# The opening in four column quarters, the rotary angles moved, later modulation pieces spread by a plan, and attention heads in two banks

## The reference, cut to what matters

```
mod = silu(c) @ ada_w[l] + ada_b[l]            # 2048 x 6144 weights per layer
shift, scale, gate = split(mod, 3)
h = rms_norm(x, norm_g[l]) * (1 + scale) + shift
z = h @ w_in[l]
q_lat, kv_lat, k_rope, mla_gate, conv_in, conv_gate = split(z)   # 512, 256, 64, 1024, 2048, 1024
q, k, v = from rms_norm(q_lat) @ w_q_up, rms_norm(kv_lat) @ w_kv_up, and rotated k_rope
attn = causal attention over 8 heads;  mla_out = attn * silu(mla_gate)
u = glu(conv_in);  u = depthwise conv, 31 taps;  layer norm, silu;  u @ w_pw;  * silu(conv_gate)
x = x + gate * (concat(mla_out, conv_out) @ w_out[l])
```

## Time and profile before

| what | value |
|---|---|
| median of 3 runs | 2290.51 us (2286.9 to 2291.76) |
| the profiled execution | 2290.56 us |
| its span, from first to last instruction | 2288.8 us |
| TensorE busy | 2152.4 us, 94% |
| VectorE busy | 1720.2 us, 75% |
| ScalarE busy | 974.0 us, 43% |
| TensorE's granted clock, mean | 0.973 of full speed |
| moved | 559.4 MB, mean 244 GB/s |

### The profile page before, as it was taken

How to read it: one execution, slowest core, us unless ns; L and a number is a source line. 1 busy time by engine, 2 the same in 40 slices (tenths; PEclk the granted TensorE clock), 3 DMA queues, 4 the chain that set the end, 5 groups by cost and what they waited for, 6 DMA issues and landing times.

```text
span 2288.8 us, 39558 instructions
## 1 busy us (share of the span) xinstructions
PE 2152.4 (94%) x15465; PEld 2040.6 (89%) x15465; DVE 1720.2 (75%) x2347; ACT 974.0 (43%) x1517; POOL 214.1 (9%) x130
## 2 busy tenths in 40 slices
PE   2389999999999999999999999989999999999997
PEld 2389997889999978999999998889999999988886
DVE  6999997797899977878866886787776666654554
ACT  2145445225544353354454444455544444433443
POOL 0000580000007600032000000000000000000000
PEclk7599999999999999999999999999999999999999
DMA  9989956796998487979937995568876555566663
GB/s 337 349 282 351 310 168 214 268 327 200 315 354 257 142 294 244 307 174 304 364 99 255 377 370 166 157 194 270 272 220 198 181 181 181 183 220 184 188 194 123
DMA packets 390355, 559.40 MB, mean 244 GB/s; under 512 B 25543, under 2 KB 316943, under 8 KB 389724
## 3 DMA queue, kind: packets, MB, share of 16 engines
q1 hardware_dynamic: 386304, 550.70, 73.2%
q0 software_dynamic: 1456, 4.28, 0.8%
q10 hardware_dynamic: 2476, 2.82, 0.4%
HBM read 555.57 MB, written 2.18 MB: 244 GB/s over the span
## 4 chain that ended last, share of the span: by engine, by line
PE 80%; DVE 7%; DMA 5%; issue 3%; ACT 3%; SPq 0%; ACTq 0%; DVEq 0%
PE gemm L1688 75%; DMA w_raw<-in_w_in 3%; DMA ada_first<-in_ada_w 2%; DVE w_lo L1161 1%; ACT w_hi L777 1%; DVE ada_even L1129 1%; PE stat L1712 1%; PE bankO L1767 1%; DVE ada_odd L1129 1%; DVE ada_acc L1148 1%; PE bankS L1873 0%; PE bankS L1874 0%; DVE scr L1201 0%; PE bankT L1778 0%; PE gemm L1955 0%
## 5 line engine op out<-in xcount | busy, mean ns | idle before, releaser
L1688 PE MATMUL gemm<-h_hi,w_hi 128*128 128x256 f32 (+1 forms) x3312 | 947.5, 286 | 24.0 <-DVE h_lo L1206 19.0
L1161 DVE TENSOR_TENSOR w_lo<-w_raw,w_hi 128x1024 fp32r<-128x1024 f32 x540 | 654.6, 1225 | 388.6 <-ACT w_hi L777 387.1
L1688 PE MATMUL gemm<-h_lo,w_hi 128*128 128x256 f32 (+1 forms) x3312 | 942.9, 285 | 0.0
L1688 PE MATMUL gemm<-h_hi,w_lo 128*128 128x256 f32 (+1 forms) x3312 | 942.8, 285 | 0.0
L777 ACT ACTIVATE w_hi<-w_raw 128x1024 fp32r<-128x1024 f32 (+1 forms) x604 | 620.3, 1041 | 689.3 <-PE gemm L1688 494.7
L1688 PEld LDWEIGHTS gemm<-h_hi,w_hi 128*128 128x128 f32 (+1 forms) x3312 | 637.9, 193 | 26.7 <-issue 22.0
L1688 PEld LDWEIGHTS gemm<-h_lo,w_hi 128*128 128x128 f32 (+1 forms) x3312 | 638.0, 193 | 0.6
L1688 PEld LDWEIGHTS gemm<-h_hi,w_lo 128*128 128x128 f32 (+1 forms) x3312 | 637.8, 193 | 0.3
L1129 DVE SCALAR_TENSOR_TENSOR ada_even<-ada_raw,c_act,ada_even 128x1024 f32<-128x1024 f32 x160 | 212.9, 1331 | 5.5 <-DMA ada_raw<-in_w_ada 2.3
L651 POOL TENSOR_TENSOR w_lo<-w_raw,w_hi 128x1024 fp32r<-128x1024 f32 x64 | 160.7, 2518 | 412.4 <-ACT w_hi L777 412.3
L1129 DVE SCALAR_TENSOR_TENSOR ada_odd<-ada_raw,c_act,ada_odd 128x1024 f32<-128x1024 f32 x128 | 171.9, 1343 | 6.0 <-DMA ada_raw<-in_ada_w 2.9
(11 more groups left out here) (333 smaller groups left out, 2680.4 us busy)
## 6 DMA issues: line engine op xcount, KB each, us to landing
w_raw<-in_w_in SPq DMA_DIRECT2D x264, 512.0 KB, 6.1
w_raw<-in_w_up SPq DMA_DIRECT2D x176, 512.0 KB, 3.6
ada_raw<-in_ada_w SPq DMA_DIRECT2D x160, 512.0 KB, 7.3
ada_raw<-in_w_ada SPq DMA_DIRECT2D x160, 512.0 KB, 6.1
w_raw<-in_w_out SPq DMA_DIRECT2D x96, 512.0 KB, 6.2
w_raw<-in_w_down SPq DMA_DIRECT2D x88, 512.0 KB, 3.7
ada_first<-in_ada_w SPq DMA_DIRECT2D x32, 512.0 KB, 8.8
ada_late<-in_w_ada SPq DMA_DIRECT2D x32, 512.0 KB, 5.2
```

The costliest lines, as they stand in the source:

```text
L1161: dve.tensor_tensor(w_lo[:, fixed % PARTS, 0:sz], w_raw[:, fixed % RAW, 0:sz], w_hi[:, fixed % PARTS, 0:sz].bitcast(F32), ALU.subtract).th ...
L1688: last = pe.matmul(half(g, k, q), left, right, start=(kt == 0 and j == 0 and (q == 0 or g.wide)), stop=(u == len(g.units) - 1 and t == nk ...
```

## The change

It has six parts.

1. Groups 0 and 1 of layer 0 are read in four quarters: 16 pieces each, a piece with 512 columns of the shift and 512 of the scale. In each quarter VectorE adds 12 pieces to `first_acc`, and TensorE takes every fourth in 8 matmuls of 16 columns (`first_piece`), then adds VectorE's sum (`first_reduce`). `first_tiles` makes the four tiles of h that these columns allow.
2. lat and krope of layer 0 become one product `first`, over k by quarters, in four PSUM banks. SP loads its weights behind each quarter of pieces.
3. ACT issues 8 further small parameter loads at the start and the other 29 after the root of the first norm (`late_consts`); the form of c for quarters is loaded behind x.
4. The rotary angles are computed behind ua.
5. The pieces of groups 2, 3 and 4 ride elsewhere: group 2 on ua and ub; groups 3 and 4 by the table `SPREAD` on kv, q, pw, outca, outcb and outm of layer 0. outm of layer 0 has one body of 8 blocks instead of a loop over 4.
6. Scores and outputs of the attentions alternate between two banks each, `wts` are made in step 0, and out2a waits by tile. The transposes of the opening use two banks in turn.

The core of the diff:

```diff
+QUARTERS = 4
+FROWS = DM // P
+BY_PE = 4
+LEAD = 3
+PAR_EARLY = 10
+SPREAD = {"kv": [1, 0, 1, 0, 1, 0, 1, 0], "q": [2, 1, 1, 1, 2, 1, 1, 1], "pw": [1] * 8,
+          "outca": [3, 2, 2, 2, 3, 2, 2, 2], "outcb": [2] * 8, "outm": [1] * 8 + [0] * 8}
...
+        score_banks = [bankS, banks_g[0][1]]
+        o_banks = [bankO, banks_g[1][1]]
...
 # SP
+            def ada_load_first(qt, j):
+                m = FROWS * qt + j
+                slot = m % FSLOTS
+                if m >= FSLOTS:
+                    if m % BY_PE == BY_PE - 1:
+                        sp.wait_ge(first_by_pe, (m - FSLOTS) // BY_PE + 1)
+                    else:
+                        sp.wait_ge(ada_used, (m - FSLOTS + 1) - (m - FSLOTS + 1) // BY_PE)
...
-            for n in range(2):
-                for j in range(AU):
...
+            for qt in range(QUARTERS):
+                for j in range(FROWS):
+                    ada_load_first(qt, j)
+                load_first(qt)
...
 # ACT
+            act.dma_start(c16_raw[:], a["c"][0].rearrange("(k j) -> k j", j=FROWS)).then_inc(c_loaded, 16)
...
             norm_root(0, scr)
...
+            tr_copy(PAR_FIRST, par[:, 0:par_first])
+            late_consts()
...
+            for qt in range(QUARTERS):
+                first_high(qt, 0)
+                first_high(qt, 1)
+                for t in range(KQ * qt, KQ * (qt + 1)):
+                    act.wait_ge(t_ready, t + 1)
+                    act.activation(h_hi[:, t, :], scr[:, t, :], ACT.Identity, bias=mod[:, 0, t:t + 1]).then_inc(h_hi_ready, 1)
+                first_high(qt, 2)
+                first_high(qt, 3)
+                if qt == 1:
+                    par_copies()
...
 # VectorE
+            for qt in range(QUARTERS):
+                for v, j in enumerate([j for j in range(FROWS) if j % BY_PE != BY_PE - 1]):
+                    if v == LEAD and qt:
+                        first_tiles(qt - 1)
+                    first_piece(qt, j)
+            first_tiles(QUARTERS - 1)
...
                 through(G["ua", l], lambda i, k: value_of_u(i, k, G["ua", l]))
+                if l == 0:
+                    rope_angles()
...
+                    if h < NHA:
+                        head_weights(2 * h)
+                        head_weights(2 * h + 1)
                     if h == NHA + 1:
                         head_low(NHA - 1)
                 if step == 1:
                     if 1 <= h <= NHA:
                         head_scaled(h - 1)
-                    if h < NHA:
-                        head_weights(2 * h)
-                        head_weights(2 * h + 1)
...
 # TensorE
+            def first_piece(qt, j):
+                m = FROWS * qt + j
...
+                pe.wait_ge(ada_loaded[slot], 16 * (m // FSLOTS + 1))
+                for t in range(2 * KQ):
+                    last = pe.matmul(first_sums(qt)[:, t * SUM_COLS:(t + 1) * SUM_COLS],
+                                     first_slot(slot)[:, 0, t * P:(t + 1) * P], c16[:, j, :],
+                                     start=(j == BY_PE - 1 and t == 0), stop=False, skip_group_check=True)
+                last.then_inc(first_by_pe, 1)
...
+            for j in by_pe:
+                first_piece(0, j)
             norm_first(scr)
...
+            first_reduce(0)
+            for qt in range(QUARTERS):
+                more = list(by_pe) if qt + 1 < QUARTERS else []
+                first_unit(qt, 0)
+                first_unit(qt, 1)
+                for j in more[0:1]:
+                    first_piece(qt + 1, j)
+                first_unit(qt, 2)
+                for j in more[1:2]:
+                    first_piece(qt + 1, j)
+                first_unit(qt, 3)
+                for j in more[2:]:
+                    first_piece(qt + 1, j)
+                if qt == 1:
+                    par_turned()
+                if more:
+                    first_reduce(qt + 1)
...
-            multiply(G["out2a"], ready=(mix_ready, lambda t: 2 * LAYERS + 2 + t // 2))
+            multiply(G["out2a"], ready=(mix_ready, lambda t: 2 * LAYERS + 2 + (t + 1) // 2), by_tile=True)
```

More of the change, by code:

```diff
@@ L407, in program @@
                             G_hi, G_lo, lambda i, k, B: (i * B + k) * WB)
+        pieces = [(n, j) for n in (3, 4) for j in range(AU)]
+        for name, counts in SPREAD.items():
+            g = G[name, 0]
+            g.ada, g.plan = None, []
+            for c in counts:
+                g.plan.append(pieces[:c])
+                pieces = pieces[c:]
+            for n, j in sum(g.plan, []):
+                if j == 0:
+                    g.zero = n
+        assert not pieces
         after = {id(g): n for g, n in zip(prods, prods[1:] + [None])}
@@ L556, in ada_pieces @@
         def ada_pieces(before, u, units):
+            if before is not None and before[0].plan is not None:
+                return [(n, j, j, AU * n + j, (AU * (n - 2) + j) // ASLOTS + 2 * AU // FSLOTS + 1)
+                        for v in units_beside(before, u, units) for n, j in before[0].plan[v]]
             if before is None or before[0].ada is None:
@@ new lines, in first_high, with first_out @@
+            def first_high(qt, b):
+                n, fixed = first.unit(0, qt, b)
+                if fixed >= PARTS:
+                    act.wait_ge(w_used, n - PARTS + 1)
+                wait_loaded(act, first, 0, qt, b)
+                sz = KQ * first_cols(b)[1]
+                act.activation(w_hi[:, fixed % PARTS, 0:sz], w_raw[:, fixed % RAW, 0:sz], ACT.Copy).then_inc(w_hi_done, 1)
+            def first_out(b):
+                wait_full(act, first, 0, b)
+                for q in range(2):
+                    if b < 3:
+                        freed(act.activation(lat[:, 2 * b + q, :], half(first, b, q), ACT.Copy), first, b)
+                    else:
+                        cols = slice(q * P, (q + 1) * P)
+                        freed(act.activation(kropeT[:, cols], half(first, b, 0)[:, cols], ACT.Copy), first, b)
@@ new lines, in _ @@
+            for qt in range(QUARTERS):
[8 more added lines that the diff above has]
+                    par_copies()
+            for b in range(4):
+                prep(G["ua", 0], 0, 0, only=b)
+                first_out(b)
@@ new lines, in first_reduce @@
+            def first_reduce(qt):
+                pe.wait_ge(ada_used, FROWS * (BY_PE - 1) // BY_PE * (qt + 1) if qt < QUARTERS - 1 else 2 * AU)
+                for t in range(2 * KQ):
+                    last = pe.matmul(first_sums(qt)[:, t * SUM_COLS:(t + 1) * SUM_COLS],
+                                     first_acc[:, qt % 2, t * P:(t + 1) * P], ones[:, 0:SUM_COLS],
+                                     start=False, stop=(t == 2 * KQ - 1), skip_group_check=True)
+                last.then_inc((first_summed, stat_ready)[qt % 2], 1)
@@ new lines, in first_unit @@
+            def first_unit(qt, b):
+                n, fixed = first.unit(0, qt, b)
+                cols = first_cols(b)[1]
+                pe.wait_ge(w_split, n + 1)
+                ws = [w[:, fixed % PARTS, 0:KQ * cols].rearrange("p (k n) -> p k n", k=KQ) for w in (w_hi, w_lo)]
+                qs = range(2 if b < 3 else 1)
+                for t in range(KQ):
+                    kt = KQ * qt + t
+                    if b == 0:
+                        pe.wait_ge(h_ready, kt + 1)
+                    for q in qs:
+                        for j, (w, x) in enumerate(((ws[0], h_hi), (ws[0], h_lo), (ws[1], h_hi))):
+                            last = pe.matmul(half(first, b, q), w[:, t, q * P:min((q + 1) * P, cols)], x[:, kt, :],
+                                             start=(kt == 0 and j == 0 and q == 0),
+                                             stop=(kt == KT - 1 and j == 2 and q == qs[-1]), skip_group_check=True)
+                last.then_inc(w_used, 1)
@@ new lines, in par_turned @@
+            def par_turned():
+                pe.wait_ge(const_loaded, 16 * n_const)
+                for b, ss_ in enumerate(((0, 1, 2), (3, 4))):
+                    dst = tr_bank(PAR_TR + b)
+                    c = 0
+                    for s in ss_:
+                        n = sum(v.shape[0] for v in par_sources[s]) // P
+                        last = pe.transpose(dst[:, c:c + n], par_rows[0:n, s, :], ident[0:n, 0:n])
+                        c += n
+                    last.then_inc(tr_ready, 1)
+                dst = tr_bank(PAR_TR + 2)
+                for l in range(LAYERS):
+                    for c in range(CT):
+                        j = (l * CT + c) * TAPS
+                        last = pe.matmul(dst[:, j:j + TAPS], dw_rows[:, l, c * P:(c + 1) * P], ident[0:TAPS, 0:TAPS],
+                                         start=True, stop=True)
+                last.then_inc(tr_ready, 1)
```

325 lines of the change are left out of this document (207 added, 118 removed).

## The result

The changed kernel takes 2323.33 us (median of 4 runs, 2321.65 to 2325.73), the kernel before 2291.03: ratio 1.0142, 95% interval 1.0127 to 1.0156. Forecast was no change, with a range up to 2303; it came 32 us slower. The profiled execution has a span of 2319.9 us against 2288.8.

What follows compares the result with a forecast made beforehand. TensorE, busy for 94% of the span, was taken as the bound, with the date of "ua" deciding. Opening +4, rotary angles +5, head weights -7 and the rest -2 summed to 0: 2290.5 us, range 2273 to 2303.

Steps and rivals of the forecast that it cites:

- Quarter 0: First quarter of the opening: root at 46, ACT free at 63, first matmul at 69, request for piece 27 at 81.
- slower rival: ACT between the root and its first w_hi: late issue stalls as before, 8.5 us more, 2299; chance 0.30.
- Quarters 1 to 3: Rest of the opening: 37 pieces 50 us, w_in 9, holds 12, last piece at 152; "ua" at 169, +4.
- 5.8 us twice: Quarters 2 and 3: SP held again, as freeing a slot takes about 16 us and eight requests last 11.
- the sum: The opening's times added up to the start of "ua": 169 against 164.8, so +4, bounds +1 to +12.
- The tail: Last piece to "ua": add 1.2, reduce 1.8, w_lo, mod and tile 2.8, 84 matmuls 10.5, ending at 169.
- outca term: Two more pieces (2.6 us) on VectorE in outca: 0 to +2 us, taken as 0.
- The plan: Pieces of groups 3 and 4 spread over kv, q, outca and outm: 0 to +2 us, taken as 0.
- Rotary angles: VectorE's angles moved to the end of "ua": reciprocal 6.1 us later, +5 us on the path, upper end 6.
- Head weights: wts a step earlier: waits of 5.4 us and 1.7 of lower clock go, -7, bounds 0 and -10.
- out2a by tiles: Of the 2.5 us wait for the last head's low part, 2 go: -2 us.
- Two banks: Attention scores and outputs: no long TensorE wait on the single banks, so 0.

Runs made afterwards that it cites:

- a_pe: The changed kernel with TensorE's pieces 3 and 7 of the next quarter ahead of the product's first unit: 2313.09 us, ratio 1.0085.
- a_issue: The changed kernel with ACT's 29 late small loads issued behind the tiles of quarter 0: 2318.84 us, ratio 1.0122.
- c_dw: The changed kernel with late loads behind quarter 0's tiles, TensorE's pieces ahead of the units, and dw_w loads split by rows: 2304.4 us, ratio 1.0052.
- c_lead: c_dw with six instead of three of VectorE's next-quarter pieces ahead of a quarter's tiles: 2297.23 us, ratio 1.0026.
- b_plan: The kernel before with only the changed plan of the later pieces, including outm's body of 8 blocks: 2310.06 us, ratio 1.0084.
- a_rope: The changed kernel with the rotary angles back in the opening, ahead of quarter 1's tiles: 2322.64 us, ratio 1.0129.
- b_heads: The kernel before with only the head weights on VectorE made a step earlier: 2286.03 us, ratio 0.9972.
- b_tile: The kernel before with only the product out2a over the upper half by tiles: 2291.77 us, ratio 0.9999.

## Why the prediction was wrong

**What bounds the kernel** was read rightly: TensorE is full behind the opening, and the date of "ua" counts. What was drawn from it was not. That a piece taken out of these stages makes nothing faster there does not mean that a piece put into the next ones costs nothing, and VectorE's time, which decides that, was reckoned for kv and outca alone.

**Quarter 0**: right. Root forecast 46, measured 46.87; ACT free at 63, measured 60.45; first matmul 69, measured 66.72; request 27 at 81, measured 76.66, with the transfers idle as forecast. No issue stood still: the longest of the late ones took 2.07 us. The stall that the prediction reckoned with as a rival did not come again: the loads of ACT's queue were slow again (alone, from 62 to 70 us, it moved 19 GB/s), but they ran in the hole, where nothing waited for them. So the slower rival, which has the right sign, has the wrong place: its condition (ACT busy past 66 us) was not met.

**Quarters 1 to 3** (+4 forecast for the opening, +17.5 measured). "ua" came at 182.0 against 169, although quarter 0 gave back 4.3 us. Three things lie between.

The step "5.8 us twice" failed in its second half. The transfers stood 7.4 and 12.9 us (last landing before the hold to first one behind it: 107.4 to 114.8, 141.3 to 154.2); without 1.36 for the landing piece itself these are 6.0, as forecast, and 11.5. Ahead of piece 51 TensorE had the transposes of the parameters and the 32 matmuls of dw (124.2 to 132.5), which the sum moved out of the opening's first part and never put back. VectorE, done with its three pieces at 131.2, waits for ACT, which copies their result first, and for TensorE's sum behind them (three rows: ACT, VectorE, VectorE):

```profile
132.59 0.58 ACT L850 ACTIVATE dwT<-bankT 128x496 f32<-128x496 f32 x1 [6.81 <-PE bankT L2040]
134.15 1.22 DVE L1293 TENSOR_TENSOR w_lo<-w_raw,w_hi 128x1024 fp32r<-128x1024 f32 x1 [2.91 <-ACT w_hi L966]
136.11 0.17 DVE L1310 TENSOR_TENSOR mod<-bankO,par 128x8 f32<-128x8 f32 x1 [0.74 <-PE bankO L2002]
```

By an estimate from these rows (131.2 and 1.2 for w_lo, against 136.1) that is 3.5 of the 5.7 us too few; the other 2 stay open.

The transfers between the holds took another 5 us more than the sum had: piece 27 landed 4.0 us after its request, piece 31 had to wait for TensorE as well (requested at 81.3), and the rest is spread. So the last piece landed at 159.7, forecast 153.

The tail took 22.2 us instead of 16. TensorE's last piece and the sum took 3.60 and 3.57 us at the lower clock (TensorE had waited 3.58 us before them), against 1.2 and 1.8 in the sum, and the 84 matmuls 12.9 against 10.5. The latter is a slip in the sum: 84 x 0.119 is 10.0, and the 5 us at the lower clock that it names add 2.5. (Two more slips decide nothing: 16 less 11 is 5.0 and not 5.8, and 2299 with the outca term is 2301 and not 2303.) a_pe, a_issue, c_dw and c_lead each took away a part of all this, and "ua" went from 182.0 to 154.4.

**The plan** (0 to +2 forecast, +18.0 measured by b_plan): this is the step that failed most. The prediction priced two extra pieces in outca and four in kv. Of the 8 in outm it asked only whether their transfers would be late, not what they cost VectorE, and the two more in q and the new due date of group 2 it passed over. Measured in the changed kernel: 9.8 us in outm, 3.6 at the end of "ub", 2.7 ahead of pw. VectorE in outm shows it, a block of the changed kernel (7.57 us; in the kernel before one takes 5.76):

```profile
551.56 0.87 DVE L1447 SCALAR_TENSOR_TENSOR xT<-gemm,mod,xT 128x256 f32<-128x256 f32 x2
553.86 1.23 DVE L1337 TENSOR_TENSOR w_lo<-w_raw,w_hi 128x1024 fp32r<-128x1024 f32 x1 [1.43 <-ACT w_hi L865]
555.00 1.28 DVE L1259 SCALAR_TENSOR_TENSOR ada_even<-ada_raw,c_act,ada_even 128x1024 f32<-128x1024 f32 x1
556.20 1.22 DVE L1337 TENSOR_TENSOR w_lo<-w_raw,w_hi 128x1024 fp32r<-128x1024 f32 x1
557.33 1.28 DVE L1259 SCALAR_TENSOR_TENSOR ada_even<-ada_raw,c_act,ada_even 128x1024 f32<-128x1024 f32 x1
```

Before the change VectorE is busy for 38.0 of the 51 us from 509 to 560, yet 1.43 us of each block are a wait for ACT's w_hi inside a chain: with it 5.3 of 5.76 us were taken. Ahead of pw the chain runs through the two more pieces of q, which stand on VectorE in front of the scaling of conv; ACT, which passes conv on to TensorE, waits for it, in the changed kernel and before:

```profile
422.61 4.04 ACT L1057 ACTIVATE conv<-conv,par 128x256 f32<-128x256 f32 x8 [2.91 <-DVE conv L1610]
394.60 4.04 ACT L927 ACTIVATE conv<-conv,par 128x256 f32<-128x256 f32 x8 [0.19 <-DVE conv L1426]
```

And group 2, whose pieces ended in "ua" before, where nobody waited for them, now ends in the last units of "ub", right ahead of its sum. Its last pieces come late from the transfers and take up to 2.92 us each, against 1.28 before GpSimd began its w_lo at 274.3 us (that GpSimd is the cause is not shown):

```profile
279.55 2.41 DVE L1259 SCALAR_TENSOR_TENSOR ada_even<-ada_raw,c_act,ada_even 128x1024 f32<-128x1024 f32 x1 [0.94 <-DMA ada_raw<-in_ada_w]
282.32 2.92 DVE L1259 SCALAR_TENSOR_TENSOR ada_even<-ada_raw,c_act,ada_even 128x1024 f32<-128x1024 f32 x1 [0.36 <-DMA ada_raw<-in_ada_w]
```

**Rotary angles** (+5 forecast): the mechanism was right, the wait 2.5 us with 1.7 more from a stretch at the lower clock (245.9 to 249.3); a_rope shows that their other place costs as much.

**Head weights** (-7): -6.3 by b_heads, right. **out2a by tiles** (-2): 0 by b_tile. **Two banks** (0): about -3, with an interval that nearly reaches zero.

By medians: +18.0 - 6.3 - 3.2 - 0.5 = +8 for the parts run alone; the other 24 of the 32 us are the opening and what follows from it, of which four edits gave back 26 (2323.3 to 2297.2; one of them, the split of dw_w, gains as much in the kernel before).

**What stays open**: 2.6 us, the difference between these 24 and the 17.5 at "ua" plus 4.2 for the rotary angles. The medians of five kernels stand in this sum, each uncertain by 2 to 3 us, and stretches at the lower clock behind short waits are of that size too. It also stays open whether the 16 displaced pieces have a place that costs less than 18 us: that was tried for 8 of them only.

## What to carry to other kernels

Work that is taken out of one place has to be priced where it lands: list every engine's chain there, and count idle time inside a chain (between two waits that hang on each other) as taken. A ring of buffers with two consumers is as slow as the later of them, and a request that waits for it holds everything behind it in the queue; put the slow consumer's part first. Before a tuned schedule is rebuilt, look for a load that stands still: here splitting two small loads won 6 us in a kernel whose new opening lost 24.
